# Turning stream chunks with two VectorE operations and four transfers, and combining a down pair's shared products at its end

## Chip, cores, metric

The kernel runs on one core of a Trainium2 chip. The metric is the device time of one execution in microseconds; the profile is one execution taken by the hardware profiler, and its span is the core's time from the first to the last instruction.

## What is computed

A two-layer decoder trunk on 256 tokens of width 2048, all in float32. Layer 0 is differential attention, layer 1 attention over a shared latent; each is followed by an MLP. Cut to what matters here:

```python
x = x + diff_attention(rms_norm(x, a_norm_g[0]), ...) # ends in "o @ w_o"
x = x + sq_relu_mlp(rms_norm(x, mlp_norm_g[0]), w_up[0], w_down[0])
k_nope, k_rope, v = shared_latent_kv(x, kv_in_norm_g, w_dkv, kv_norm_g, w_ukv, cos_b, sin_b)
x = x + mla_attention(rms_norm(x, b_norm_g[0]), ...) # ends in "o @ w_o"
x = x + sq_relu_mlp(rms_norm(x, mlp_norm_g[1]), w_up[1], w_down[1])
return rms_norm(x, final_norm_g)

def sq_relu_mlp(h, w_up, w_down):
    return jnp.square(jax.nn.relu(h @ w_up)) @ w_down
```

## The kernel before

**Products.** Every float32 factor is split in two parts of fewer bits, high and low, and a product is three matmuls: high by high, high by low, low by high (`half_tok`, lines 582 to 584; in `seven`, lines 815 to 817). ScalarE writes the high parts of the weights (`whi`, line 1067), VectorE the low ones (`wlo`, line 1669) from what SyncE's queue loads into the four slots of `raw`. A *block* is 2048 rows by 512 columns of weights; it is cut into eight *halves* of 256 rows, each 12 matmuls of 512 columns (two chunks, two token tiles, three products). `whi` and `wlo` form a ring of four halves. ScalarE may split half hf once TensorE has done half hf - 4, VectorE follows ScalarE, TensorE waits for VectorE (`lo_ready`), and a slot of `raw` is loaded again once VectorE has split it. `body(b, asides)` is the loop that both engines run over the splits: half 3 of block b to half 2 of the next, numbered 3 to 10; `asides` says after which of them other work stands.

**The MLP.** Its 8192 hidden columns are done in four quarters of four up blocks and four down blocks. The sums go to the PSUM tiles `acc`; the squares of the result are turned to become the next operand (`opB`). In all quarters but the edges, blocks 2 and 3 of a down projection (`pair`) and pairs of up blocks (`up_pair`) form part of the result with seven products instead of eight (`seven`, names `B22`, `T1`, `B21`, `B11`, `T2`, `T3`, `T4` in this order, 6 matmuls each). These need sums of weights, which VectorE forms (lines 2197, 2200, 2207, 2213), and their high and low parts (`extra_hi`, `extra_lo`, lines 1389, 1393, 2180, 2186). Four products are shared between results and go to the `side` banks; ScalarE copies them out (lines 1414 for a down pair, 1440 for an up pair), and VectorE combines them with four operations (`combine`, line 2103). For a down pair the result is then scaled and added to the stream `xs` (`down_add`, line 2251, two operations of 1024 columns). The order in one quarter is: down blocks 0 and 1, `pair`, first `up_pair`, second `up_pair`. In the second one, VectorE has the squares of the first to sum and turn (lines 2109, 2117, 2085) and their low parts to write (`hid_low`, line 2093) between the seven products' parts; ScalarE squares (lines 1352, 1360, 1347), moves the turned quadrants with four transfers (`move_quads`, line 1333) and writes high parts (line 1323).

**Stream chunks.** The stream `xs` has tokens on the partitions; the next projection needs it with features there. After a block of an output projection or of the last down projection has been added to `xs` (line 2060, or 2134), its 512 columns (a *chunk*) are turned. VectorE's `transpose` turns squares of 32 by 32, so `turn` (line 1690) issues one operation for each pair of 32-partition groups, 16 a chunk; `x_turn` does them in three parts of 4, 8 and 4, the first behind the addition, the others behind the splits of halves 3 and 4 of the next block (`x_turned_over`). Then, behind half 6, ScalarE writes the chunk's high part to `opA` (`x_hi`, lines 1098 and 1101) and VectorE the low part (`x_lo`, lines 1709 and 1714). There are twelve chunks: four for each output projection and four for layer 0's last down projection. The last chunk of each four is wanted by TensorE at half 6 of the block that follows (`opA_ready`): the first up block of either layer, and the latent projection `B_DKV`.

```python
for a in tokens:
    for c in range(4):
        rows, cols = (slice(32 * k, 32 * k + 32) for k in (a, c))
        done = nc.vector.transpose(
            dest[cols].rearrange("p f (t n) -> p f t n", t=TT)[:, :, :, rows],
            src[rows].rearrange("p t (f n) -> p f t n", f=4)[:, :, :, cols])
```

Of the kernel before, what the change touches and what calls it, by code (L numbers as in the profile page):

```python
# [159 lines left out]
def trunk(nc, x, positions, a_w_qkv, a_lambda, a_w_o, w_dkv, w_ukv, b_w_dq, b_w_uq, b_w_o, w_up, w_down,  # L160
# [11 lines left out]
    with ExitStack() as ctx:  # L172
# [81 lines left out]
        x_turned = o_sb[:].rearrange("p a t n -> p (a t) n")  # L254
        squares = junk[:].rearrange("p a n -> p (a n)").rearrange("p (q c r) -> p q c r", c=4, r=32)
        sq_quads = o_sb[:].rearrange("p a t n -> p (a t n)")
        sq_moved = prob[:].rearrange("p m k -> p (m k)")[:, 0:4 * SEQ].rearrange("p (t a x) -> p t a x", t=TT, a=4)
        sqT = sq_moved.rearrange("p t a (f n) -> p f (t a) n", f=4)
# [55 lines left out]
        x_turns = sem("x_turns")  # L314
        xT_hi = sem("xT_hi")
# [723 lines left out]
        def _(act):  # L1039
# [267 lines left out]
            def out_proj(b0, uses, v0, gain):  # L1307

                x_squares(v0, 1, uses[1] + 1)
                for j in range(1, JB):  # L1310
                    s = (j + 1) % 2
                    body(b0 + j, {6: lambda: x_hi(v0 + j - 1, gain)})
# [4 lines left out]
            def mlp(l, v_in, v_out, nxt, squares_from):  # L1317
# [8 lines left out]
                def move_quads(q, j):  # L1326
# [5 lines left out]
                    for a in range(4):  # L1332
                        act.dma_start(sq_moved[:, :, a, :], sq_quads[32 * a:32 * a + 32, :]).then_inc(sq_moves, 16)  # L1333
# [63 lines left out]
                def pair(q):  # L1397
# [9 lines left out]
                    for hf in range(3):  # L1407
                        split(b + 2, hf)

                def up_pair(q, i, after):  # L1410

                    b = B_MLP[l] + 2 * JB * q + 2 * i
                    def down_copy(k):
                        fn(down_shared[k], side[k], ACT.Copy).then_inc(shared_copied, 1)

# [3 lines left out]
                    elif after == "down":  # L1419
                        down_copy(0)  # L1420
# [3 lines left out]
                    elif after == "down":  # L1424
                        down_copy(1)
# [33 lines left out]
                body(B_MLP[l], {6: lambda: x_hi(v_in + JB - 1, G_MLP[l]), 9: lambda: form_high(x_forms[0], FORM_SETS * l)})  # L1459
# [1093 lines left out]
```

## Time and profile before

| | |
|---|---|
| median of 3 runs (lowest to highest) | 1999.61 us (1997.5 to 1999.82) |
| the profiled execution | 1997.04 us, span 1995.2 us |
| TensorE matmul / weight load busy | 99% / 83% |
| VectorE / ScalarE busy | 82% / 58% |
| DMA | 398.91 MB, mean 200 GB/s |
| granted TensorE clock | 0.999 |

Busy time of a matmul overlaps the next one's, and its end is modelled: a 512-column matmul is shown with 0.39 us while the next starts 0.23 us after it. Idle time is therefore read from the starts.

### The profile page before, as it was taken

To read this page: it belongs to the slowest core of one execution; us is meant where nothing else is said; L and a number is where in the kernel's file an instruction comes from. 1 tells how busy PE (TensorE), PEld (TensorE's weight loads), DVE (VectorE), ACT (ScalarE), POOL (GpSimd) and SP (SyncE) were. 2 spreads that over 40 slices of the span, in tenths; PEclk is the share of its full clock that TensorE was granted. 3 is DMA by queue.
4 is the path that set the end of the run, shared out by engine and by line. 5 is a ranking of instruction groups with operands and counts; after the bars stand their busy time and mean duration, and the time that the engine had idled before them with its cause. 6 is when DMAs were issued, how large, how long until landed. Compare 5 with 4: busy or idle time off the path is not lost.

```text
span 1995.2 us, 26053 instructions
## 1 busy us (share of the span) xinstructions
PE 1981.0 (99%) x9128; PEld 1649.4 (83%) x9128; DVE 1636.8 (82%) x2099; ACT 1155.7 (58%) x1481; POOL 13.2 (1%) x21
## 2 busy tenths in 40 slices
PE   9999999999999999999999999999999999999998
PEld 7888888888888888888878998888887888888887
DVE  7789998977887898788788787977798788789865
ACT  6555555556566556556646665556456556655653
POOL 0000000000000000000000000000000000000000
PEclk9999999999999999999999999999999999999999
DMA  8655545566666566656655554576556656655673
GB/s 309 208 171 188 187 157 181 201 205 227 210 204 214 195 205 225 220 203 196 231 190 173 142 151 148 184 232 216 182 196 227 228 203 207 219 193 200 220 238 108
DMA packets 252861, 398.91 MB, mean 200 GB/s; under 512 B 17648, under 2 KB 75376, under 8 KB 252784
## 3 DMA queue, kind: packets, MB, share of 16 engines
q1 hardware_dynamic: 217104, 379.03, 56.8%
q10 hardware_dynamic: 35680, 18.88, 3.5%
q8 instruction: 44, 0.72, 0.1%
q14 instruction: 33, 0.27, 0.0%
HBM read 379.00 MB, written 2.10 MB: 191 GB/s over the span
## 4 chain that ended last, share of the span: by engine, by line
PE 80%; DVE 8%; issue 5%; ACT 3%; ACTq 2%; DMA 1%; SPq 0%; DVEq 0%; POOLq 0%; POOL 0%
PE acc L582 20%; PE acc L584 20%; PE acc L583 20%; PE acc L602 2%; PE acc L604 2%; PE acc L603 2%; DVE wlo L1669 2%; PE side L815 2%; PE side L817 2%; PE side L816 2%; ACTq L1333 2%; DVE wlo L2186 1%; PE acc L815 1%; PE acc L817 1%; PE acc L816 1%
## 5 line engine op out<-in xcount | busy, mean ns | idle before, releaser
L1669 DVE TENSOR_TENSOR wlo<-raw,whi 128x1024 fp32r<-128x1024 f32 (+1 forms) x596 | 708.1, 1206 | 158.8 <-ACT whi L1067 156.7
L1067 ACT ACTIVATE whi<-raw 128x1024 fp32r<-128x1024 f32 (+1 forms) x596 | 608.3, 1044 | 392.0 <-PE acc L584 267.4
L582 PE MATMUL acc<-whi,opB 128*128 128x512 f32 x1104 | 431.1, 390 | 1.3 <-DVE wlo L1669 1.2
L584 PE MATMUL acc<-whi,opB 128*128 128x512 f32 x1104 | 429.8, 389 | 0.0
L583 PE MATMUL acc<-wlo,opB 128*128 128x512 f32 x1104 | 429.5, 389 | 0.0
L582 PE MATMUL acc<-whi,opA 128*128 128x512 f32 (+2 forms) x1072 | 414.7, 387 | 0.0
L584 PE MATMUL acc<-whi,opA 128*128 128x512 f32 (+2 forms) x1072 | 414.0, 386 | 0.0
L583 PE MATMUL acc<-wlo,opA 128*128 128x512 f32 (+2 forms) x1072 | 413.8, 386 | 0.0
L582 PEld LDWEIGHTS acc<-whi,opB 128*128 128x128 f32 x1104 | 207.3, 188 | 44.8 <-DVE wlo L1669 2.4
L584 PEld LDWEIGHTS acc<-whi,opB 128*128 128x128 f32 x1104 | 207.2, 188 | 43.3
L583 PEld LDWEIGHTS acc<-wlo,opB 128*128 128x128 f32 x1104 | 207.3, 188 | 42.7
L584 PEld LDWEIGHTS acc<-whi,opA 128*128 128x128 f32 x1072 | 201.3, 188 | 40.3
L582 PEld LDWEIGHTS acc<-whi,opA 128*128 128x128 f32 x1072 | 201.3, 188 | 40.1 <-issue 0.4
L583 PEld LDWEIGHTS acc<-wlo,opA 128*128 128x128 f32 x1072 | 201.4, 188 | 39.8
L1393 ACT ACTIVATE whi<-raw 128x1024 fp32r<-128x1024 f32 x78 | 82.6, 1059 | 79.5 <-issue 28.7
L2186 DVE TENSOR_TENSOR wlo<-raw,whi 128x1024 fp32r<-128x1024 f32 x78 | 95.1, 1220 | 16.6 <-ACT whi L1393 16.6
L1389 ACT ACTIVATE extra_hi<-raw 128x1024 fp32r<-128x1024 f32 x52 | 54.7, 1051 | 74.1 <-PE side L817 74.1
L1690 DVE STREAM_TRANSPOSE o_sb<-xs 32x256 f32<-32x256 f32 x192 | 83.8, 436 | 3.3
L2085 DVE STREAM_TRANSPOSE o_sb<-junk 128x1024 f32<-128x1024 f32 x32 | 39.8, 1245 | 44.1 <-ACT junk L1347 43.8
L2180 DVE TENSOR_TENSOR extra_lo<-raw,extra_hi 128x1024 fp32r<-128x1024 f32 x52 | 63.5, 1221 | 13.8 <-ACT extra_hi L1389 13.6
L602 PE MATMUL acc<-whi,opA 128*128 128x512 f32 x184 | 71.8, 390 | 0.2 <-DVE wlo L1669 0.2
L603 PE MATMUL acc<-wlo,opA 128*128 128x512 f32 x184 | 71.7, 389 | 0.0
(379 smaller groups left out, 2431.1 us busy)
## 6 DMA issues: line engine op xcount, KB each, us to landing
raw<-in_w_up SPq DMA_DIRECT2D x128, 1024.0 KB, 5.4
raw<-in_w_down SPq DMA_DIRECT2D x128, 1024.0 KB, 5.0
raw<-in_a_w_qkv SPq DMA_DIRECT2D x44, 1024.0 KB, 5.1
raw<-in_a_w_o SPq DMA_DIRECT2D x16, 1024.0 KB, 5.0
prob<-o_sb ACTq DMA_DIRECT2D x128, 128.0 KB, 2.9
raw<-in_b_w_o SPq DMA_DIRECT2D x16, 1024.0 KB, 5.0
raw<-in_w_ukv SPq DMA_DIRECT2D x32, 256.0 KB, 4.1
raw<-in_w_dkv SPq DMA_DIRECT2D x4, 1024.0 KB, 5.0
```

What stands on the lines that cost most here:

```text
L582: mm(o, a_hi, w_hi, start=start, stop=False)
L583: mm(o, a_hi, w_lo, start=False, stop=False)
L584: done = mm(o, a_lo, w_hi, start=False, stop=last and c == chunks - 1)
L602: mm(o, a_hi, whi[:, place, :], start=start, stop=False)
L603: mm(o, a_hi, wlo[:, place, :], start=False, stop=False)
L815: mm(o, a_hi, hi[:, place + c, :], start=first and c == 0, stop=False)
L1067: done = fn(whi[:, place:place + ch, 0:n], raw[:, r, c0:c0 + ch, 0:n], ACT.Copy)
L1393: fn(whi[:, 2 * (hf % 4):2 * (hf % 4) + 2, :], source[f], ACT.Copy).then_inc(hi_ready, 1)
L1669: done = tt_(wlo[:, place:place + ch, 0:n], raw[:, r, c0:c0 + ch, 0:n], whi[:, place:place + ch, 0:n].bitcast(F32), ALU.subtract)
L1690: done = nc.vector.transpose(dest[cols].rearrange("p f (t n) -> p f t n", t=TT)[:, :, :, rows], src[rows].rearrange("p t (f n) -> p f t n" ...
L2180: tt_(extra_lo[:, places, :], src, extra_hi[:, places, :].bitcast(F32), ALU.subtract).then_inc(extra_lo_ready, 1)
L2186: tt_(wlo[:, places, :], src, whi[:, places, :].bitcast(F32), ALU.subtract).then_inc(lo_ready, 1)
```

## The change

A chunk is now turned by two VectorE operations over all 128 partitions, one for each token tile. They turn every 32 by 32 square in its place of four partition groups and read `xs` with a step of four columns, so that each group of 32 partitions ends up with whole quadrants (`quads`, in `o_sb`). Four transfers issued by ScalarE (`x_move`) bring the groups to their columns in `prob` (`quads_moved`, read as `sqT`), the same way and through the same two buffers as the hidden squares are moved. High and low parts read from there. All of the turning stands behind the addition; `x_move` stands behind half 4 and the high and low parts behind half 7 (in block 1 of the last down projection behind 7 and 10). In the first up block the high and low parts of the forms of `x` go to the block after.

The four copies of a down pair's shared products are issued behind the second of the three splits that end `pair`, no longer between the splits of the next up pair. VectorE's `combine` stands at the end of `pair`, ahead of the last addition, and `down_add` behind the first sum of the next up pair, ahead of the split of half 4.

```diff
+            def x_move(v):
+
+                act.wait_ge(x_turns, v - JB + 1)
+                act.wait_ge(xT_lo, 4 * v)
+                for a in range(4):
+                    act.dma_start(quads_moved[:, :, a, :], quads[32 * a:32 * a + 32, :]).then_inc(x_moves, 16)
+
             def x_hi(v, gain):
 
-                act.wait_ge(x_turns, v - JB + 1)
+                act.wait_ge(x_moves, 64 * (v - JB) + 64)
                 c = JB * (v % JB)
+                high = opA[:, c:c + 4, 0, :].rearrange("p f (a n) -> p f a n", n=32)
                 if gain is None:
-                    fn(opA[:, c:c + 4, 0, :], x_turned, ACT.Copy).then_inc(xT_hi, 4)
+                    fn(high, sqT, ACT.Copy).then_inc(xT_hi, 4)
                     return
                 for k in range(4):
-                    fn(opA[:, c + k, 0, :], x_turned[:, k, :], ACT.Copy,
+                    fn(high[:, k], sqT[:, k], ACT.Copy,
                        scale=gains[:, gain + c + k:gain + c + k + 1]).then_inc(xT_hi, 1)
...
                     seven(down_groups(l, q, 1), 2, b + 1, 2, (1, b + 1), (2, b + 1), {})
                     split(b + 1, 6)
                     split(b + 1, 7)
-                    for hf in range(3):
-                        split(b + 2, hf)
+                    split(b + 2, 0)
+                    split(b + 2, 1)
+                    for k in range(4):
+                        fn(down_shared[k], side[k], ACT.Copy).then_inc(shared_copied, 1)
+                    split(b + 2, 2)
...
                     split(b, 5)
-                    if after == "down":
-                        down_copy(2)
-                    else:
+                    if after != "down":
                         move_quads(q, 2 * i - 1)
-                    between = {"B22": lambda: down_copy(3)} if after == "down" else {
-                        "B21": lambda: hid_high(q, 2 * i - 1)}
+                    between = {} if after == "down" else {"B21": lambda: hid_high(q, 2 * i - 1)}
...
-            def x_turn(v, tokens, s, added):
+            def x_turn(v, s, added):
 
                 dve.wait_ge(drained[s], added)
+                if not (isinstance(v, int) and v == JB):
+                    dve.wait_ge(x_moves, 64 * (v - JB))
                 j = v % JB
-                done = turn(x_turned, xs[:, :, NB * j:NB * j + NB], tokens)
-                if 3 in tokens:
-                    done.then_inc(x_turns, 1)
+                for t in range(TT):
+                    done = nc.vector.transpose(
+                        quads.rearrange("p (c t f n) -> p t f c n", c=4, t=TT, n=32)[:, t],
+                        xs[:, t, NB * j:NB * j + NB].rearrange("p (f r c) -> p f c r", f=4, c=4))
+                done.then_inc(x_turns, 1)
...
+                    combine(down_shares(l, q), down_shared)
                     add_scaled(b + 1, 0, 2 * uses[0], slice(3 * NB, 4 * NB))
...
                 def down_add(q):
 
                     dve.wait_ge(shared_sums, 4 * down_shares(l, q) + 4)
+                    for side_bank in range(2):
+                        dve.wait_ge(drained[side_bank], 2 * (u[side_bank] + U_QUARTER * q + U_UP + 2))
...
-                        if follows != "down":
+                        if follows == "down":
+                            down_add(q - 1)
+                        else:
                             up_turn(q, 2 * i - 1)
...
-                    split(b + 1, 2)
-                    if follows == "down":
-                        down_add(q - 1)
-                    for hf in range(3, 6):
+                    for hf in range(2, 6):
                         split(b + 1, hf)
                     combine(up_shares(l, q, i), up_shared)
...
-                body(B_MLP[l], {**x_turned_over(v_in + JB - 1, G_MLP[l], 0, 2 * u[0]),
-                                7: lambda: stream_stats(2 * l + 1, True), 8: x_form_sums,
-                                10: lambda: form_low(x_forms, FORM_SETS * l)})
-                body(B_MLP[l] + 1, {3: lambda: up_turn(0, 0), 6: lambda: hid_low(0, 0)})
+                body(B_MLP[l], {7: lambda: x_lo(v_in + JB - 1, G_MLP[l]), 8: lambda: stream_stats(2 * l + 1, True),
+                                9: x_form_sums})
+                body(B_MLP[l] + 1, {3: lambda: up_turn(0, 0), 4: lambda: form_low(x_forms, FORM_SETS * l), 6: lambda: hid_low(0, 0)})
```

TensorE's instructions and their order are the same in both kernels. On VectorE, around the addition of block 1 of layer 0's last down projection (`xs<-acc`), before:

```order
L2134 SCALAR_TENSOR_TENSOR xs<-acc,rs,xs 128x512 x2
L1690 STREAM_TRANSPOSE o_sb<-xs 32x8x32 x4
L1669 TENSOR_TENSOR wlo<-raw,whi 128x1024
L1690 STREAM_TRANSPOSE o_sb<-xs 32x8x32 x8
L1669 TENSOR_TENSOR wlo<-raw,whi 128x1024
L1690 STREAM_TRANSPOSE o_sb<-xs 32x8x32 x4
L1669 TENSOR_TENSOR wlo<-raw,whi 128x1024 x2
L1709 TENSOR_TENSOR opA<-o_sb,opA 128x4x256
L1669 TENSOR_TENSOR wlo<-raw,whi 128x1024 x4
```

and now:

```order
L2135 SCALAR_TENSOR_TENSOR xs<-acc,rs,xs 128x512 x2
L1704 STREAM_TRANSPOSE o_sb<-xs 128x4x4x32 x2
L1671 TENSOR_TENSOR wlo<-raw,whi 128x1024 x5
L1715 TENSOR_TENSOR opA<-prob,opA 128x4x256
L1671 TENSOR_TENSOR wlo<-raw,whi 128x1024 x3
```

The 16 transposes between splits have become two behind the addition, and the low part of the chunk (`opA`) stands one split later. On VectorE at the end of a down pair and in the up pair behind it (`o_sb<-o_sb,junk` is the first of the four combining operations, `xs<-junk` and `xs<-o_sb` are the two additions of the combined products, `attn_both<-raw` is the first sum), before:

```order
L1669 TENSOR_TENSOR wlo<-raw,whi 128x1024
L2131 ISA
L2134 SCALAR_TENSOR_TENSOR xs<-acc,rs,xs 128x512 x2
L1657 ISA
L1669 TENSOR_TENSOR wlo<-raw,whi 128x1024
...
L2197 TENSOR_TENSOR attn_both<-raw 128x1024
...
L2097 ISA
L2103 TENSOR_TENSOR o_sb<-o_sb,junk 128x512
...
L1669 TENSOR_TENSOR wlo<-raw,whi 128x1024
L2251 SCALAR_TENSOR_TENSOR xs<-junk,rs,xs 128x1024
L2251 SCALAR_TENSOR_TENSOR xs<-o_sb,rs,xs 128x1024
```

and now:

```order
L1671 TENSOR_TENSOR wlo<-raw,whi 128x1024
L2098 ISA
L2104 TENSOR_TENSOR o_sb<-o_sb,junk 128x512
...
L2132 ISA
L2135 SCALAR_TENSOR_TENSOR xs<-acc,rs,xs 128x512 x2
L1659 ISA
L1671 TENSOR_TENSOR wlo<-raw,whi 128x1024
...
L2198 TENSOR_TENSOR attn_both<-raw 128x1024
L2247 ISA x2
L2250 SCALAR_TENSOR_TENSOR xs<-junk,rs,xs 128x1024
L2250 SCALAR_TENSOR_TENSOR xs<-o_sb,rs,xs 128x1024
```

The combining has moved ahead of the last addition from `acc`, and the two additions from behind the seven products' parts to behind the first sum. On ScalarE at the same place (`junk<-side` and `o_sb<-side` are the copies), before:

```order
L1067 ACTIVATE whi<-raw 128x1024
L1414 ACTIVATE junk<-side 128x512
L1056 REGISTER_ALU
L1067 ACTIVATE whi<-raw 128x1024
L1414 ACTIVATE junk<-side 128x512
L1056 REGISTER_ALU
L1067 ACTIVATE whi<-raw 128x1024
L1414 ACTIVATE o_sb<-side 128x512
```

and now:

```order
L1067 ACTIVATE whi<-raw 128x1024
L1056 REGISTER_ALU
L1067 ACTIVATE whi<-raw 128x1024
L1418 ACTIVATE junk<-side 128x512 x2
L1418 ACTIVATE o_sb<-side 128x512 x2
L1056 REGISTER_ALU
L1067 ACTIVATE whi<-raw 128x1024
```

The four copies now stand together ahead of one split.

## Rows read from the trace of the kernel before

**Rows 1.** The page, busy time by engine; then the waits of TensorE (total, times, longest).

```profile
PE 1981.0 (99%) x9128; PEld 1649.4 (83%) x9128; DVE 1636.8 (82%) x2099; ACT 1155.7 (58%) x1481; POOL 13.2 (1%) x21
...
PE side L815 <- DVE wlo L2186: 3.7, 6, 0.6
PE acc L582 <- DVE wlo L1669: 1.2, 1, 1.2
```

**Rows 2.** Timeline, TensorE, last down projection of layer 0 (start, duration, operation).

```profile
1031.29 0.39 PE L583 MATMUL acc<-wlo,opB 128*128 128x512 f32 x1
1031.52 0.39 PE L584 MATMUL acc<-whi,opB 128*128 128x512 f32 x1
1033.09 0.50 PE L582 MATMUL acc<-whi,opB 128*128 128x512 f32 x1 [1.18 <-DVE wlo L1669]
...
1035.71 0.39 PE L584 MATMUL acc<-whi,opB 128*128 128x512 f32 x1
1036.17 0.50 PE L582 MATMUL acc<-whi,opB 128*128 128x512 f32 x1
```

**Rows 3.** Timeline, VectorE, the same stretch.

```profile
1028.21 3.58 DVE L1690 STREAM_TRANSPOSE o_sb<-xs 32x256 f32<-32x256 f32 x8
1031.80 1.23 DVE L1669 TENSOR_TENSOR wlo<-raw,whi 128x1024 fp32r<-128x1024 f32 x1
...
1034.89 2.36 DVE L1669 TENSOR_TENSOR wlo<-raw,whi 128x1024 fp32r<-128x1024 f32 x2
```

**Rows 4.** Timeline, TensorE, second up pair of quarter 1, layer 0.

```profile
612.81 0.40 PE L817 MATMUL acc<-whi,opA 128*128 128x512 f32 x1
613.16 0.50 PE L815 MATMUL side<-extra_hi,opA 128*128 128x512 f32 x1
...
614.45 0.39 PE L817 MATMUL side<-extra_hi,opA 128*128 128x512 f32 x1
615.43 0.50 PE L815 MATMUL side<-whi,q_parts 128*128 128x512 f32 x1 [0.60 <-DVE wlo L2186]
615.77 0.39 PE L816 MATMUL side<-wlo,q_parts 128*128 128x512 f32 x1
```

**Rows 5.** Timeline, VectorE, both up pairs of that quarter.

```profile
575.23 1.28 DVE L2251 SCALAR_TENSOR_TENSOR xs<-o_sb,rs,xs 128x1024 f32<-128x1024 f32 x1
...
579.84 0.69 DVE L2103 TENSOR_TENSOR junk<-junk 128x512 f32<-128x512 f32 x1
...
622.95 0.69 DVE L2103 TENSOR_TENSOR junk<-junk 128x512 f32<-128x512 f32 x1 [0.72 <-ACT prob L1440]
```

**Rows 6.** Timeline, ScalarE, last copy of shared products in either up pair.

```profile
578.80 0.61 ACT L1440 ACTIVATE prob<-side 128x512 f32<-128x512 f32 x1
...
622.31 0.61 ACT L1440 ACTIVATE prob<-side 128x512 f32<-128x512 f32 x1
```

**Rows 7.** Groups of instructions (line, shapes, busy us and mean ns, idle before).

```profile
L1690 DVE STREAM_TRANSPOSE o_sb<-xs 32x256 f32<-32x256 f32 x192 | 83.8, 436 | 3.3
L2085 DVE STREAM_TRANSPOSE o_sb<-junk 128x1024 f32<-128x1024 f32 x32 | 39.8, 1245 | 44.1 <-ACT junk L1347 43.8
...
L1352 ACT ACTIVATE junk<-o_sb 128x1024 f32<-128x1024 f32 x14 | 28.8, 2054 | 27.0 <-DVE o_sb L2109 27.0
```

**Rows 8.** Timeline, TensorE, first matmul of the first up pair.

```profile
550.14 0.39 PE L582 MATMUL acc<-whi,opA 128*128 128x512 f32 x1
```

**Rows 9.** Timeline, VectorE, start of the first up pair.

```profile
550.51 1.41 DVE L2134 SCALAR_TENSOR_TENSOR xs<-acc,rs,xs 128x512 f32<-128x512 f32 x2 [0.56 <-PE acc L584]
...
554.38 1.23 DVE L2197 TENSOR_TENSOR attn_both<-raw 128x1024 f32<-128x1024 f32 x1 [1.33 <-DMA raw<-in_w_up]
```

**Rows 10.** Instructions on tile prob: the transfers, durations min/median/max.

```profile
L1333 ACTq DMA_DIRECT2D prob<-o_sb x128: 617/642/1553, 407.6 to 1911.8; - x128
...
DMA to landing us min/median/max: 2.6/2.9/6.0
```

**Rows 11.** The page, costliest groups: ScalarE's high parts.

```profile
L1067 ACT ACTIVATE whi<-raw 128x1024 fp32r<-128x1024 f32 (+1 forms) x596 | 608.3, 1044 | 392.0 <-PE acc L584 267.4
```

More of the change, by code:

```diff
@@ L314, in trunk @@
         x_turns = sem("x_turns")
+        x_moves = sem("x_moves")
         xT_hi = sem("xT_hi")
@@ L1311, in out_proj @@
                     s = (j + 1) % 2
-                    body(b0 + j, {6: lambda: x_hi(v0 + j - 1, gain)})
+                    body(b0 + j, {4: lambda: x_move(v0 + j - 1), 7: lambda: x_hi(v0 + j - 1, gain)})
                     x_squares(v0 + j, s, uses[s] + j // 2 + 1)
@@ L1418, in up_pair @@
                         square_second(q, i - 1)
-                    elif after == "down":
-                        down_copy(0)
                     split(b, 4)
@@ L1526, in latent_hi @@
                        scale=gains[:, gain + c:gain + c + 1]).then_inc(latT_hi, 1)
-            body(B_DKV, {6: lambda: x_hi(V_MLP0 + JB - 1, None)}, kind="dkv", nxt="rq")
+            body(B_DKV, {4: lambda: x_move(V_MLP0 + JB - 1), 7: lambda: x_hi(V_MLP0 + JB - 1, None)}, kind="dkv", nxt="rq")
             latent(0, B_DKV, 1, stage, KV_LORA, 0)
@@ L1693, in turn @@
                 return done
-            def x_turn(v, tokens, s, added):
+            def x_turn(v, s, added):
                 dve.wait_ge(drained[s], added)
+                if not (isinstance(v, int) and v == JB):
+                    dve.wait_ge(x_moves, 64 * (v - JB))
                 j = v % JB
-                done = turn(x_turned, xs[:, :, NB * j:NB * j + NB], tokens)
-                if 3 in tokens:
-                    done.then_inc(x_turns, 1)
+                for t in range(TT):
[3 more added lines that the diff above has]
+                done.then_inc(x_turns, 1)
             def x_lo(v, gain):
-                dve.wait_ge(x_turns, v - JB + 1)
                 c = JB * (v % JB)
+                high, low = (opA[:, c:c + 4, i, :].rearrange("p f (a n) -> p f a n", n=32) for i in range(2))
                 if gain is None:
                     dve.wait_ge(xT_hi, 4 * v + 4)
-                    tt_(opA[:, c:c + 4, 1, :], x_turned, opA[:, c:c + 4, 0, :].bitcast(F32),
-                        ALU.subtract).then_inc(xT_lo, 4)
+                    tt_(low, sqT, high.bitcast(F32), ALU.subtract).then_inc(xT_lo, 4)
                     return
@@ L1713, in x_lo @@
                     dve.wait_ge(xT_hi, 4 * v + k + 1)
-                    stt(out=opA[:, c + k, 1, :], in0=x_turned[:, k, :], scalar=gains[:, gain + c + k:gain + c + k + 1],
-                        in1=opA[:, c + k, 0, :].bitcast(F32), op0=ALU.mult, op1=ALU.subtract).then_inc(xT_lo, 1)
-            def x_turned_over(v, gain, s, added):
-                return {3: lambda: x_turn(v, (1, 2), s, added), 4: lambda: x_turn(v, (3,), s, added),
-                        6: lambda: x_lo(v, gain)}
+                    stt(out=low[:, k], in0=sqT[:, k], scalar=gains[:, gain + c + k:gain + c + k + 1],
+                        in1=high[:, k].bitcast(F32), op0=ALU.mult, op1=ALU.subtract).then_inc(xT_lo, 1)
             def stream_stats(t, squared):
@@ L2207, in seven @@
                     tt_(b22, w_sum, b22, ALU.add).then_inc(w_summed, 1)
-                    if "third sum" in after:
-                        after["third sum"]()
                     low("B21", group, at, b, hf0, b21)
@@ L2268, in up_pair @@
                     after = {"first sum": after_first, "second sum": lambda: split(b, 5)}
-                    if follows == "down":
-                        after["third sum"] = lambda: down_combine(q - 1)
-                    else:
+                    if follows != "down":
                         after["B11"] = lambda: hid_low(q, 2 * i - 1)
                     seven(up_groups(l, q, i), i - 1, b, 6, (3, b), (0, b + 1), 8 * b + 3, after)
-                    split(b + 1, 2)
-                    if follows == "down":
-                        down_add(q - 1)
-                    for hf in range(3, 6):
+                    for hf in range(2, 6):
                         split(b + 1, hf)
```

43 lines of the change are left out of this document (18 added, 25 removed).

## Prediction

> **What bounds the kernel now.** I read the page first and then every wait of TensorE, because an engine that is busy 99% of the span leaves others almost nothing to give [rows 1]. TensorE's waits in total come to under 7 us in 1995.2: six of 0.6 us on VectorE's line 2186 and one of 1.2 us on line 1669 carry nearly all of it [rows 1]. So the question is not how much work the change takes off VectorE, but what it does to these seven places and whether it makes a new one.
>
> Busy time hides short holes, so I took the starts of the matmuls in TensorE's timeline. A 512-column matmul starts 0.23 us after the one before. I list every step longer than 0.30 us; beyond the regular 0.23 they add up to 11.1 us, in two kinds of place that the change touches, with 8.3 us, and in the start and the attention stages, which it leaves alone.
>
> The first kind is one place, in the third column block of layer 0's last down projection. The matmul after 1031.52 starts 1.57 us later, so 1.34 are lost; a half further on 0.46 lie between two starts, so 0.23 [rows 2]. After such a hole the next step is also 0.33 to 0.34 long instead of 0.23, as [rows 4] show. Together 1.34 + 0.23 + 2 x 0.1 = 1.8 us. The cause is in VectorE's timeline: eight transposes of 32 partitions run from 1028.21, and the low parts (line 1669) that TensorE wants start only at 1031.80; the next pair of them stands behind four more transposes, at 1034.89 [rows 3].
>
> The second kind occurs six times, once for each quarter but the last in each layer, in the second up pair. There TensorE loses 0.12 us at the product B11 (612.81 to 613.16), 0.75 us at T2 (614.45 to 615.43), and 0.11 us in the step behind each (615.43 to 615.77) [rows 4]: 1.1 us each time, 6.5 in all.
>
> I followed the chain of waits back from this hole: VectorE's own operations, ScalarE behind four transfer issues, the sums and squares of the pair before, and so on to line 2103 at 579.84 [rows 5], where VectorE puts together the shared products of the first up pair. That operation is the anchor. ScalarE's last copy of those products ends at 578.80 + 0.61 = 579.41 [rows 6], but VectorE starts only at 579.84, since its three splits are behind the two additions of line 2251, the second of which starts at 575.23 [rows 5]. In the second up pair, where no such additions stand ahead, the same operation starts at 622.95, 0.03 after its last copy's end at 622.31 + 0.61 = 622.92, and the row says that it waited for this copy [rows 5, 6].
>
> **The change, part by part.** *Turning a stream chunk.* Twelve chunks are turned. Before, each took 16 transposes of 436 ns: 192 of them, 83.8 us [rows 7]. Now each takes two of 128 x 512. The trace has none; the nearest is line 2085, 128 x 1024 in 1245 ns [rows 7], half of which is 0.62. The new ones read their source with a step of four elements. Line 1352 reads so on ScalarE and takes 2054 ns for 1024 columns [rows 7], where two copies of 512 take 0.61 each [rows 6], so the upper bound is twice, 1.25. I take 0.62, because the nearest row is the same operation: 24 x 0.62 = 15 us (30 at the upper bound), 69 us less on VectorE. Of this only the hole of 1.8 us is on the path. The low parts at 1031.80 have no transposes ahead of them any more except two right behind the additions, so both that hole and the one behind it go: **minus 1.8 us**.
>
> *The four transfers.* Each chunk adds four issues on ScalarE, 0.64 us each, and they land 2.9 us after the issue (median; 6.0 at most) [rows 10]. The 48 issues hold ScalarE 31 us in all. They lie behind the split of half 4, and each block gives ScalarE 8 halves x 12 matmuls x 0.227 = 21.8 us for 8 splits of 1.04 [rows 11], squares and one high part, so 2.6 us more are covered. The Trainium skill, DMA: Bandwidth & Descriptors, Issuing engines are not separate DMA queues, has the issuing time as usually small relative to the DMA itself; the trace does not agree here, 2.6 us of issues against a landing of 2.9, and by that rule the risk that the issues hold the splits up would be none. What could be late is the high part, moved from half 6 to 7, and the low part behind it. TensorE needs the last chunk at half 6 of the following block, 16.3 us after the block's start, in three places only (the first up block of both layers and the latent projection). Split 7 can start when four halves are done, at 10.9; the split ends at 12.0, the high parts at 13.7 and the low parts at about 15.2 (my estimate: one operation of 1024 columns takes 1.04 and 1.23 us [rows 3, 11], and cut in four some 1.7). The transfers are issued by 7.2 and landed by 10, with the slowest landing by 12.6. So about 1 us is left: **0**. If the slowest landing fell there, it would cost half a us at one place.
>
> *The shared products of the down pair.* ScalarE's four copies, VectorE's four combining operations (4 x 0.69 = 2.8 us) and two additions (1.28 each) leave the middle of the first up pair. The combining goes ahead of the pair's last addition, the two additions behind the first sum. The total work stays, so the gain is one of order. From the anchor on nothing is ahead of line 2103 but ScalarE's copies, so it starts at 579.44 and the chain behind it is 0.40 earlier. Each link further down is an operation that waits for the one before (VectorE, ScalarE, issues), none for TensorE. The weights that the next first sum wants are fetched when a split of the same chain frees their slot, so they come earlier too. T2's hole shrinks by what the chain gains; TensorE arrives 0.23 earlier as B11's hole goes. Hence 1.1 becomes 0.7, and 6 x 0.40 = **minus 2.4 us**. Bounds: 0, if another releaser ends the chain's waits at the same time as now, and 6.5, if all of the holes go.
>
> *What stands in the way at the pair's start.* VectorE is free at 549.95 (it idles 0.56 before 550.51) [rows 9], and the copies delay its third split by about 0.15. Then come combining 2.8, an addition 1.33, a split 1.14: it reaches the first sum at 555.4, after the weights for which it waited until 554.38 [rows 9]. So the idle time of 1.33 there is the cover. With the sum (1.14), the two additions (2.4) and a split of 1.22 the low parts of half 4 are ready at 560.1. TensorE starts the block at 550.14 [rows 8] and comes to half 4 after 4 x 12 x 0.23 = 11.0 us, at 561.2. The margin is 1.1 us; every later half has more. **0**.
>
> *Moved in the first up block.* The forms' high and low parts (1.05 and 1.2 us) go one block later, where drain and first move have slack: 0.
>
> **Sum.** 1.8 + 2.4 = 4.2 us off the profiled execution, 1997.04, gives 1992.8. The median of the three runs shown is 1999.61, 2.6 above that execution; against it the forecast is 1995.4. A measurement of this kernel tells about 0.2% (4.0 us) from no change, so the forecast lies right at this edge.
>
> **Rivals.**
> *Only the chunk's hole goes (1997.8).* For: two transfers' landings and a weight fetch lie in the chain beside the operations, and if either does not come 0.40 earlier, nothing is gained. Against: the DMA issues follow the chain's own operations. 13%.
> *All holes go (1991.3).* 8.3 us, if the chain comes earlier by over 1 us, as it would where ScalarE, without copies between its splits, runs ahead more than I see. Against: the anchor waits for TensorE's seven products and cannot be earlier than 579.4. 12%.
> *A new wait at the pair's start (2003.8, slower).* The place is half 4 of the first up pair. The price is 6 times what VectorE is late beyond 1.1 us; 0.7 us too late eats the gain (6 x 0.7 = 4.2), and from there the kernel is slower. If the first sum's weights land at 557.8 instead of 554.4 [rows 9], half 4 is ready at 562.6, 1.4 too late: 6 x 1.4 = 8.4, less 4.2. For: the cover at this place, 1.33 us of idle time, is used up. Against: the split that frees the weights' slot stands ahead of the combining, so nothing postpones their fetch. 7%.
> *The change doesn't do what it says (1999.6).* ScalarE is held in `x_move` by the issues and by waiting for the transposes, and splits fall behind by as much as VectorE got ahead. For: four issues of 0.64 stand in a queue that splits share. Against: ScalarE sits idle for 267 us of the span in front of its splits, waiting for TensorE to free their places [rows 11]. 6%.
> *VectorE was the bound (1931).* TensorE's weight loads are busy 83% and VectorE 82% [rows 1]; were the matmuls stretched by waiting inside their busy time, the 69 us would come off in full. Against: the starts are 0.23 apart with holes of 11.1 us in all. 2%. The Trainium skill, Perfetto Trace Analysis, Identifying the Most-Contended Engine, has matmul busy time as a bad measure and weight-load busy share as the good one for the room left; by that rule TensorE has room and the time would be nearer to 1931, and here the starts of the matmuls decide against it.
>
> **From cases to numbers.** The forecast gets 60%. It lies at the edge and three runs scatter by 2.3 us, so I split it 35 to 25 over faster and same. Faster: 35 + 12 + 2 = 49%. Same: 25 + 13 + 6 = 44%. Slower: 7%. The range reaches from the case in which all holes go, 1991.3, to just above the case in which only the chunk's hole goes, 1999.0; outside are the slower case, the one without effect, VectorE's and some scatter, 2 in 10.
>
> **What would show it.** Right: no step over 0.30 us near 1031; 24 transposes of 128 x 512 at 0.62 to 1.25; the combining of the first up pair starts 0.03 after the fourth copy; T2's wait is about 0.45 instead of 0.60 by the profile, and B11's step is back at 0.23. Wrong: a wait of TensorE on line 1671 at half 4 of the first up pair or at half 6 of a block that takes a chunk; T2's hole unchanged or gone.

## The result and the profile after

The changed kernel takes 2003.6 us (median of 8 runs, 2002.84 to 2005.96) against 1999.11 for the kernel before (8 runs, 1997.5 to 1999.82) on the same chip. The ratio is 1.0024, 95% interval 1.0014 to 1.0033. It is slower by 4.5 us, where 1995.4 was forecast. The profiled execution took 2005.96 us, its span is 2004.2.

The page's lines on the span, on busy time and on queue q14 (packets, MB, share of 16 engines), kernel after:

```profile
span 2004.2 us, 25960 instructions
...
PE 1985.4 (99%) x9128; PEld 1653.1 (82%) x9128; DVE 1578.2 (79%) x1931; ACT 1156.6 (58%) x1481; POOL 13.2 (1%) x21
...
q14 instruction: 42, 0.34, 0.0%
```

VectorE lost 168 instructions, as planned, and 58.6 us of work, where the prediction had 69 [rows 1]. The time rose. TensorE's waits say where, kernel after:

```profile
PE acc L582 <- DVE opB L2094: 4.4, 2, 2.2
PE side L815 <- DVE wlo L2187: 3.7, 6, 0.6
...
PE side L815 <- DVE extra_lo L2181: 0.8, 1, 0.8
PE acc L582 <- DVE wlo L1671: 0.7, 2, 0.4
```

The 1.2 us on the chunk's low parts [rows 1] is gone. The six waits at T2 are all there and as long as before, which the prediction had named as a sign of being wrong. New are two waits of 2.2 us for `opB` (line 2094, `hid_low`). They stand in layer 0, at the start of the second and the third pass of the loop over the quarters. TensorE's timeline at the first of them, kernel after:

```profile
647.76 0.39 PE L584 MATMUL acc<-whi,opB 128*128 128x512 f32 x1
650.38 0.49 PE L582 MATMUL acc<-whi,opB 128*128 128x512 f32 x1 [2.23 <-DVE opB L2094]
...
651.63 0.62 PE L584 MATMUL acc<-whi,opB 128*128 128x512 f32 x1
652.05 0.63 PE L582 MATMUL acc<-whi,opB 128*128 128x512 f32 x1
...
654.61 0.60 PE L582 MATMUL acc<-whi,opB 128*128 128x512 f32 x1
655.04 0.40 PE L583 MATMUL acc<-wlo,opB 128*128 128x512 f32 x1
```

The step is 2.62 instead of 0.23. From 651.63 to 655.04 eight steps are 0.43 long instead of 0.23: behind the idle time TensorE ran for 3.4 us at the lower of its two levels, 1.2 GHz. That costs another 8 x 0.2 = 1.6. The windows view (span, then busy time of the engines; the seventh figure is the granted clock, then DMA share and GB/s) shows it too:

```profile
640.00:660.00 20.00, 17.46 (x69) 13.66 (x68) 10.22 (x10) 10.03 (x11) 0.00 (x0) 0.91 0.56 174
```

All steps over 0.30 us ("long steps" from here on), beyond 0.23 each and without those of the first 20 us, add up to 19.4 us after and 11.1 before. The two places hold 4.6 + 4.6 = 9.2 of it. Of the rest, 1.8 us went near 1031 and 0.9 came in the second up pairs. These 8.3 us account for the two profiled executions, which lie 8.9 apart (1997.04 and 2005.96); the medians lie only 4.5 apart, because the one profiled execution is 2.1 below its median and the other 2.4 above. What differs between an execution and its median, no trace shows.

**Why VectorE is late there.** Its timeline, kernel after:

```profile
637.07 1.23 DVE L1671 TENSOR_TENSOR wlo<-raw,whi 128x1024 fp32r<-128x1024 f32 x1 [1.76 <-ACT whi L1067]
642.66 0.69 DVE L2118 TENSOR_TENSOR attn_both<-acc,attn_both 128x512 f32<-128x512 f32 x1 [4.36 <-PE acc L584]
```

The same two instructions in the kernel before:

```profile
636.61 1.23 DVE L1669 TENSOR_TENSOR wlo<-raw,whi 128x1024 fp32r<-128x1024 f32 x1 [1.75 <-ACT whi L1067]
637.75 0.68 DVE L2117 TENSOR_TENSOR attn_both<-acc,attn_both 128x512 f32<-128x512 f32 x1
```

The low part is the last operation of a pass, the sum (line 2118) the first of the next: between them VectorE jumps back (line 2291). Before, the jump cost nothing (1.14 from start to start, as between any two such operations). Now VectorE does nothing from 638.3 to 642.66. The row puts this on TensorE's `acc`. The chain that ended last tells it otherwise (start, length, what; `DVEq` is VectorE's own handling of register and branch instructions), kernel after:

```profile
635.98 1.07 ACT whi L1067
...
637.16 0.07 DVEq L2291
637.23 5.18 issue
642.41 0.09 DVEq L2291
...
642.66 0.70 DVE attn_both L2118
```

"issue" is time in which the engine waited for nothing that the profile shows. The branch of the jump runs at 637.16, and the next instruction, a register operation that needs nothing of TensorE, only at 642.41. The DMA view of 636 to 652 us has one queue more than that of the kernel before:

```profile
q14 instruction: 3, 0.02, 0.5%
```

In this window the kernel before has no such packet. Queue q14 brings instructions, 8 KB in a packet (0.34 MB in 42 of them; before 33). The three lie at 640.6, 643.0 and 645.5 us, about 2.5 us apart. The work after the jump is a chain of sum, squares, turning, transfers, high and low part, and everything in it is late by the pause. At 812.5 us it happens again; in layer 1, whose loop has the same body, it doesn't (1568.61 to 1569.75).

### The profile page after: what moved, and what is told of

Same layout as the page of the kernel before. It is cut to its first block, busy times and chain, and to the rows that moved or that the text cites. A ratio compares the mean times of both kernels' runs of the same rounds, so it can differ in the third digit from the quotient of the medians.

```text
span 2004.2 us, 25960 instructions
## 1 busy us (share of the span) xinstructions
PE 1985.4 (99%) x9128; PEld 1653.1 (82%) x9128; DVE 1578.2 (79%) x1931; ACT 1156.6 (58%) x1481; POOL 13.2 (1%) x21
## 4 chain that ended last, share of the span: by engine, by line
PE 83%; ACT 4%; issue 4%; DVE 4%; DMA 2%; ACTq 2%; SPq 0%; DVEq 0%; POOLq 0%; POOL 0%
PE acc L582 20%; PE acc L584 20%; PE acc L583 20%; PE side L815 2%; PE side L816 2%; PE side L817 2%; PE acc L602 2%; PE acc L603 2%; PE acc L604 2%; DMA prob<-o_sb 2%; ACTq L1341 2%; PE acc L815 2%; PE acc L817 2%; PE acc L816 1%; ACT whi L1067 1%
## 5 line engine op out<-in xcount | busy, mean ns | idle before, releaser
L602 PE MATMUL acc<-whi,opA 128*128 128x512 f32 x184 | 71.8, 390 | 0.2 <-DVE wlo L1671 0.2
L604 PE MATMUL acc<-whi,opA 128*128 128x512 f32 x184 | 71.7, 390 | 0.0
```

The lines of the kernel that those rows point to most:

```text
L602: mm(o, a_hi, whi[:, place, :], start=start, stop=False)
L604: done = mm(o, a_lo, whi[:, place, :], start=False, stop=end)
```

## The experiments

**Theory 1**: at the jump back part of VectorE's loop is no longer in its instruction store (the place from which the engine reads its program) and is fetched again. The change put the loop elsewhere, because 16 transposes a chunk became 2 and all instructions behind them moved up. **Theory 2**: the change's own work (four copies, combining, transfers at other places) makes VectorE late. In each experiment both kernels ran on one chip; "before" is its median there. Line numbers of the variants are shifted by a few.

| kernel | us (runs) | before, us (runs) | ratio, 95% interval |
|---|---|---|---|
| changed + 24 memsets | 1994.69 (11) | 1998.76 (26) | 0.998, 0.9971 to 0.9989 |
| before + 72 memsets | 2014.93 (5) | 1998.76 (26) | 1.0077, 1.0063 to 1.0091 |
| down pair's part only | 1997.27 (11) | 1998.76 (26) | 0.9991, 0.9982 to 1.0 |
| chunks' part only | 2004.25 (10) | 1998.76 (26) | 1.0025, 1.0015 to 1.0034 |
| chunks' part + 24 memsets | 1997.02 (11) | 1999.1 (16) | 0.9989, 0.998 to 0.9998 |
| before + 36 memsets | 2008.19 (5) | 1999.45 (13) | 1.0046, 1.0032 to 1.0059 |
| changed, loop written out | 1994.46 (9) | 1999.45 (13) | 0.9977, 0.9967 to 0.9987 |
| changed + 24, low part later | 1991.14 (5) | 1999.45 (13) | 0.9961, 0.9947 to 0.9974 |
| changed + 24, both later | 1989.9 (5) | 1999.45 (13) | 0.9951, 0.9938 to 0.9965 |
| before, both later | 1993.26 (6) | 1999.1 (16) | 0.997, 0.9958 to 0.9982 |
| changed, loop written out, both later | 1989.96 (5) | 1999.1 (16) | 0.9952, 0.9938 to 0.9966 |

### The changed kernel, moved by 24 places

```diff
             nc.vector.memset(junk[:, 0, 0:P], 0.0).then_inc(zeros_ready, 1)
+            for k in range(24):
+                nc.vector.memset(junk[:, 1, k:k + 1], 0.0)
             for c in range(FIRST):
```

> The changed kernel with 24 one-column memsets at the start of VectorE's program, so that every later instruction of VectorE stands 24 places further on. Theory 1 (code fetch): VectorE's loop over the quarters has about 277 instructions, and where it stands decides how much of it has to be fetched again at the jump back; TensorE waits 2.2 us for VectorE there, twice, and runs at the lower clock behind it, about 9 us together. 24 places further on the two waits are gone: 2003.6 - 9 = 1994.6 us, no packets of the instruction queue between 600 and 840 us. Theory 2 (the work): the waits come from what the change does in the second up pair (four copies, combining, transfers at other places); 24 memsets alter none of it: 2003.6.

Measured: 1994.69 us, 8.9 less than the changed kernel. The two were not measured side by side; each against the kernel before on its own chip, one is 4.5 above and the other 4.1 below, 8.6 apart. Its two longest waits of TensorE in the waits view, and the page's line on its instruction queue:

```profile
PE side L815 <- DVE wlo L2189: 3.6, 6, 0.6
PE side L635 <- DVE junk L1826: 1.1, 1, 1.1
```

```profile
q14 instruction: 32, 0.26, 0.0%
```

The two waits of 2.2 are gone, and no instruction packet lies between 602 and 843 us. Added instructions that do nothing useful made the kernel faster by 9 us. Theory 2 cannot say why.

### The kernel before, moved by 72 places

The same edit with 72 memsets in the kernel before.

> The kernel before, its work as it was, with 72 memsets at the start of VectorE's program, so that layer 0's loop over the quarters begins at place 660 where it began at 588 (in the changed kernel at 532; 660 is 532 + 128). Theory 1 (code fetch, in blocks of 128 instructions): the kernel before gets the two waits at the jump back too: 1999.1 + 9 = 2008, with packets of the instruction queue at 640 to 650 us and at 815 to 825. Theory 2 (the work): no part of the change is in it, so 1999.1 and at most 1 more for the memsets.

Measured: 2014.93 us, 16.2 more. The waits of TensorE:

```profile
PE acc L582 <- DVE opB L2095: 8.9, 4, 2.2
PE side L815 <- DVE wlo L2188: 3.7, 6, 0.6
PE acc L582 <- DVE wlo L1669: 2.2, 4, 1.2
```

Theory 1 holds: the old work, at another place, gets the same wait. The forecast of 2008 missed, since there are four waits and not two: layer 1's loop has them as well. My places were the cause of the miss. They were taken from the program's listing, in which a loop has 276 instructions and begins at 532 or 588. The trace's own records of VectorE, register and semaphore instructions included, have 299 from one jump back to the next, 301 with the change. Beginnings of the loops worked out from these records replace the others from here on.

### The two parts of the change, each alone

`down_only` has the diff's changes in `pair`, `up_pair` and `down_add`, and the old turning of chunks; `chunks_only` is the rest of the diff: `x_turn`, `x_move`, `x_hi`, `x_lo` and their places.

> Only the down pair's part of the change: the four copies at the pair's end, the combining ahead of the last addition, the two additions behind the first sum. Layer 0's loop begins where it began before (place 588). Theory 1 (code fetch): no wait at the jump back; T2's hole stays as it is since the transfers of the chain land no earlier: 1998.5 to 1999.5. Rival, forecast as the new wait at the pair's start: if this part is what costs, 2003 to 2005 here. My term of minus 2.4 would give 1996.7.

> Only the stream chunks' part of the change (two transposes and four transfers a chunk, forms one block later); the shared products as before. Layer 0's loop begins at place 532 as in the changed kernel. Theory 1 (code fetch): the two waits at the jump back come with this part, and the hole near 1031 goes: 1999.1 + 9 - 1.8 = 2006.3, or with the changed kernel's 2003.6 if the down pair's part gives anything. If the down pair's part were the cause instead: 1997.3.

Measured: 1997.27 and 2004.25 us. TensorE's longest waits, of `down_only` and then of `chunks_only`:

```profile
PE side L815 <- DVE wlo L2179: 3.5, 6, 0.6
PE acc L582 <- DVE wlo L1662: 1.2, 1, 1.2
```

```profile
PE acc L582 <- DVE opB L2101: 4.5, 2, 2.3
PE side L815 <- DVE wlo L2194: 3.6, 6, 0.6
PE side L815 <- DVE extra_lo L2188: 1.9, 4, 0.7
```

The down pair's part costs nothing. It gives 1.5 us, between the 2.4 of my term and the 0.3 and less of theory 1's expectation, and the interval holds both. The two waits come with the chunks' part, which changes no instruction of the second up pair.

### The chunks' part, moved by 24 places

> Only the stream chunks' part of the change, with the 24 memsets, so that no loop begins where four blocks are needed (592 and 1368 of VectorE's stream, 80 and 88 modulo 128). My term for this part, the hole near 1031: 1.8 us off, so 1999.0 - 1.8 = 1997.2, and no wait at the jump back. If the four transfers or the later high and low parts cost something of their own, it is over 1999.

Measured: 1997.02 against 1999.1, so 2.1 less; no wait for `opB` is left. The interval reaches from 0.4 to 4.0 us, and it holds the term of 1.8. The trace shows the hole near 1031 gone, but not that it is the whole effect: the profiled execution took 1997.53, against 1997.04 before, and the long steps of the six second up pairs are 8.7 us, against 7.0 before. In these pairs B11's step is 0.56 to 0.83 long, where it was 0.34 to 0.37 in five of six before; why, no run shows.

With the down pair's 1.5 the medians make 3.6, where the changed kernel with 24 memsets has 4.1 less than before. So the medians add up within what can be measured. The long steps in the second up pairs do not: 7.0 before, 6.8 with the down pair's part, 8.7 with the chunks' part and 24 memsets, 6.2 with both parts and 24 memsets, each by one profile.

### Where a loop may begin

> The kernel before with 36 memsets. By the records of the traces layer 0's loop over the quarters takes 299 instructions, layer 1's as many, and they begin at 625 and 1510 of VectorE's stream (in the changed kernel 568 and 1347). If instructions are fetched in blocks of 128 of which three stay, a loop of 299 needs four blocks for 43 of 128 beginnings. Beginnings modulo 128 so far: 46, 56, 57 with waits at the jump back; 65, 67, 80, 91, 102, 104, 113 without. Here they are 21 (layer 0) and 10 (layer 1). By this model layer 0 gets two waits and layer 1 none: 1998.8 + 8 = 2007. If it is the sheer number of added instructions: four waits, 2013. If it is the alignment that the changed kernel happens to share with the 72 memsets alone: 1998.8.

Measured: 2008.19, 8.7 more. VectorE at the first jump back of layer 0, then of layer 1:

```profile
637.17 1.23 DVE L1669 TENSOR_TENSOR wlo<-raw,whi 128x1024 fp32r<-128x1024 f32 x1 [1.75 <-ACT whi L1067]
643.90 0.69 DVE L2119 TENSOR_TENSOR attn_both<-acc,attn_both 128x512 f32<-128x512 f32 x1 [5.50 <-issue]
...
1570.62 1.23 DVE L1669 TENSOR_TENSOR wlo<-raw,whi 128x1024 fp32r<-128x1024 f32 x1 [1.75 <-ACT whi L1067]
1571.77 0.68 DVE L2119 TENSOR_TENSOR attn_both<-acc,attn_both 128x512 f32<-128x512 f32 x1
```

Layer 0 has the pause and layer 1 has none, as the model of blocks says. Here the profile itself names "issue" in place of TensorE. All beginnings together:

| kernel | layer 0: begins, mod 128, waits | layer 1: begins, mod 128, waits |
|---|---|---|
| before | 625, 113, 0 | 1510, 102, 0 |
| changed | 568, 56, 2 | 1347, 67, 0 |
| changed + 24 | 592, 80, 0 | 1371, 91, 0 |
| before + 72 | 697, 57, 2 | 1582, 46, 2 |
| before + 36 | 661, 21, 2 | 1546, 10, 0 |
| down pair only | 625, 113, 0 | 1512, 104, 0 |
| chunks only | 568, 56, 2 | 1345, 65, 0 |
| chunks + 24 | 592, 80, 0 | 1369, 89, 0 |

Waits come at 21, 46, 56 and 57 and at none of 10 and 65 to 113. A loop of 299 to 301 needs four blocks of 128 instructions for 42 to 44 of 128 beginnings and three for the others (the forecast above says 43). One stretch of that width, which begins between 14 and 21, fits all sixteen. That a packet of 8 KB holds 128 instructions is inferred too: the kernel with the loop written out (below) has 404 instructions more in VectorE's program than the changed kernel with 24 memsets, and three packets more, 35 against 32, so about 135 each. The model rests on its fit and on the one forecast above, not on a view of the store.

The Trainium skill, Advanced Engine Details and Errata, ISA Cache, has the instruction cache as 32 KB in two lines of 256 instructions each. By it a loop of 299 to 301 would need a third line for 42 to 44 of 256 beginnings. The trace does not agree. Modulo 256 the beginnings with waits are 56, 185, 46 and 149, and no stretch of 44 holds them. The packets carry 8 KB, not 16. The total of 32 KB would fit four blocks of 8 KB, if three stay while a fourth is being fetched; no run shows how many the store holds.

### The loop written out

```diff
-                with dve.Fori(0, QUARTERS - 1) as q:
+                for q in range(QUARTERS - 1):
```

> The changed kernel, no memsets, with VectorE's loop over the quarters written out three times for each layer, so that its stream has no jump back there (the other engines keep theirs). Theory 1 (code fetch at the jump back): a stream that only runs forward is fetched ahead in time; no waits at 640 and 815 us: 1994.7. Theory 2 (the work): 2003.6. If fetching itself is too slow even forward, more and scattered waits: over 2003.6.

Measured: 1994.46. The place of the former jump back, VectorE's timeline:

```profile
637.31 1.23 DVE L1671 TENSOR_TENSOR wlo<-raw,whi 128x1024 fp32r<-128x1024 f32 x1 [1.76 <-ACT whi L1067]
638.45 0.68 DVE L2118 TENSOR_TENSOR attn_both<-acc,attn_both 128x512 f32<-128x512 f32 x1
```

1.14 again, and no pause of this kind is left. The forward stream was fetched in time: its 35 instruction packets, against the changed kernel's 42, cost TensorE nothing. So here the fetch costs only where it begins after the jump. Writing the loop out also takes register instructions away (VectorE's records fall from 3103 to 2327), so this run alone would not tell these from the jump; the runs with memsets do, since they keep all of them.

### The hole at T2

The other miss is T2's hole, which did not shrink. VectorE and TensorE in the changed kernel with 24 memsets (`extra_lo` is B11's low part, `opB` is `hid_low`, `wlo` T2's low part; line 815 opens B11 and then T2):

```profile
611.98 1.23 DVE L2183 TENSOR_TENSOR extra_lo<-raw,extra_hi 128x1024 fp32r<-128x1024 f32 x1 [0.23 <-ACT extra_hi L1397]
...
613.12 1.22 DVE L2096 TENSOR_TENSOR opB<-prob,opB 128x1024 fp32r<-128x1024 f32 x1
...
613.25 0.50 PE L815 MATMUL side<-extra_hi,opA 128*128 128x512 f32 x1
...
614.25 1.22 DVE L2189 TENSOR_TENSOR wlo<-raw,whi 128x1024 fp32r<-128x1024 f32 x1
...
615.53 0.51 PE L815 MATMUL side<-whi,q_parts 128*128 128x512 f32 x1 [0.62 <-DVE wlo L2189]
```

TensorE starts B11 when its low part ends. T2's low part ends two operations later, 2 x 1.14 = 2.3 us. TensorE has six matmuls in between, the first with the long step: 1.5. The difference, 0.8, is the hole, whatever the chain in front does, as long as B11's low part comes no earlier than TensorE.

> The changed kernel with the 24 memsets, and in each second up pair VectorE's low part of the moved quadrants (hid_low) stands behind the low part of T4, no longer between those of B11 and T2. Theory A: T2's hole of 0.6 is the time of this operation, since VectorE has three operations from B11's low part to T2's (3 x 1.14 us from start to end of the third) against TensorE's six matmuls, whenever the first of them comes late; so the six holes at T2 go: 1994.7 - 6 x 0.7 = 1990.5, with B11's step as it is. Theory B (the chain as I forecast it: T2 waits for whatever the whole chain releases last, here the transfers' landing): a hole of the same size stays at T2 or moves to T3 or T4: 1994.7.

```diff
                    low("B11", group, at, b, hf0, b11)
-                    if "B11" in after:
-                        after["B11"]()
                    low("T2", group, at, b, hf0, b22)
...
                    low("T4", group, at, b, hf0, w_sum)
+                    if "T4" in after:
+                        after["T4"]()
...
-                        after["B11"] = lambda: hid_low(q, 2 * i - 1)
+                        after["T4"] = lambda: hid_low(q, 2 * i - 1)
```

Measured: 1991.14, which is 3.6 below the same kernel without this edit on another chip, and 4.2 if each is taken against the kernel before on its own chip. The same stretch now:

```profile
611.85 1.23 DVE L2183 TENSOR_TENSOR extra_lo<-raw,extra_hi 128x1024 fp32r<-128x1024 f32 x1 [0.34 <-ACT extra_hi L1397]
612.99 1.22 DVE L2189 TENSOR_TENSOR wlo<-raw,whi 128x1024 fp32r<-128x1024 f32 x1
...
613.13 0.50 PE L815 MATMUL side<-extra_hi,opA 128*128 128x512 f32 x1
...
614.39 0.40 PE L817 MATMUL side<-extra_hi,opA 128*128 128x512 f32 x1
614.62 0.40 PE L815 MATMUL side<-whi,q_parts 128*128 128x512 f32 x1
```

From 614.39 to 614.62 it is 0.23: the hole is gone. The long steps of the seven products in the six second up pairs fall from 6.2 us to 2.1. Theory A holds: no step at T2 is long any more, and what is left stands mostly at B11 and the product before it in layer 1's first pass.

> As low_later, and ScalarE's high part of the moved quadrants (hid_high) stands behind the high part of T2, no longer behind that of B21, so that ScalarE doesn't wait for the landing of the transfers ahead of B11. Theory A: B11's step of 0.31 to 0.54 and the one behind it go too: 1990.5 - 6 x 0.3 = 1988.7. If the landing had nothing to do with B11's late parts: as low_later.

```diff
-                    between = {} if after == "down" else {"B21": lambda: hid_high(q, 2 * i - 1)}
+                    between = {} if after == "down" else {"T2": lambda: hid_high(q, 2 * i - 1)}
```

Measured: 1989.9, 1.2 over what was expected. The six pairs' long steps are 1.4 us, nearly all in layer 1's first. Against the run without this edit that is 1.2 less with overlapping intervals, so what the edit adds isn't settled.

### The same idea without the change, and a version without places

> The kernel before, without any part of the change, with hid_high behind T2's high part on ScalarE and hid_low behind T4's low part on VectorE in each second up pair. If T2's holes come from this order alone and not from what the change moves, they go here as well: 6.9 us of long steps in the six pairs fall to about 1.4, 1999.0 - 5.5 = 1993.5. If the earlier combining of the change is needed for that: 1997 or more.

Measured: 1993.26. What the two moved operations give (5.8 us) doesn't need the change. The six pairs' long steps are 1.9 us, where 1.4 was expected, and no wait at T2 is left. All long steps together fall from 11.1 to 6.2, so they account for 4.9 of the 5.8.

> The changed kernel with VectorE's loop over the quarters written out (no memsets) and both parts of the quadrants later. Nothing depends on where the loop begins, and the holes at T2 are gone: 1994.5 - 4.8 = 1989.7. Below both kernels, by 14 us and 9 us.

Measured: 1989.96 us (1989.5 to 1990.39), 9.1 below the kernel before and 13.6 below the changed one (measured on another occasion). Its waits of TensorE, all of them:

```profile
PE side L635 <- DVE junk L1826: 1.1, 1, 1.1
PE side L815 <- DVE extra_lo L2181: 0.6, 1, 0.6
PE acc L602 <- DVE wlo L1671: 0.3, 1, 0.3
```

## Why the prediction was wrong, step by step

Two steps failed. The sum had no term for the place of the code behind the removed instructions, which cost 8.9 us and made the kernel slower instead of faster. And T2's hole did not shrink as the chain came earlier: its six waits stayed at 0.6 each, where the term took 0.40 off each of six holes. Step by step:

**What bounds the kernel** held: TensorE's few waits, not VectorE's busy share, set the time. 58.6 us less work on VectorE gave no more than the holes. But six waits on line 2186 and one on line 1669 do not carry "nearly all" of the waits: they are 3.7 + 1.2 = 4.9 of 6.7 us, and one of 1.1 on line 1825 stands beside them.

**Turning a chunk, minus 1.8** held as far as it can be told: the hole is gone from the trace, and 2.1 was measured alone (0.4 to 4.0). The transposes were mis-sized:

```profile
L1704 DVE STREAM_TRANSPOSE o_sb<-xs x24: 1049/1092/1120, 316.4 to 1312.8; 128x512 f32<-128x512 f32 x24
```

1.09 us each where I took 0.62; the bound of 1.25 held. Whether the step of four or a fixed part in each operation makes the difference wasn't tried. It opened no hole near 1031, where the whole effect was expected.

**The four transfers, 0** held as far as TensorE's waits tell: none names `opA` in the changed kernel. The prediction's 2.6 us of issues against a landing of 2.9 set four issues beside one landing. One against one it is 0.64 to 2.9 [rows 10], so this row is not at odds with the page that the prediction cites there.

**The down pair, minus 2.4**: the size can't be told from what was measured (1.5, interval 0 to 3.6), but the place was wrong. What was foreseen at the anchor came: the combining started 0.04 after the fourth copy's end (579.40 + 0.61 = 580.01), row of the kernel after:

```profile
580.05 0.69 DVE L2104 TENSOR_TENSOR junk<-junk 128x512 f32<-128x512 f32 x1 [0.72 <-ACT prob L1441]
```

From that copy's start the transfers were issued 602.47 - 579.40 = 23.07 us later, against 602.25 - 578.80 = 23.45 before: 0.38 earlier, as forecast. But the high part that waits for their landing started 610.34 - 579.40 = 30.94 later, against 609.73 - 578.80 = 30.93 [rows 6]. ScalarE's row, before and then after:

```profile
609.73 1.06 ACT L1323 ACTIVATE opB<-prob 128x1024 fp32r<-128x1024 f32 x1 [1.66 <-DMA prob<-o_sb]
```

```profile
610.34 1.06 ACT L1331 ACTIVATE opB<-prob 128x1024 fp32r<-128x1024 f32 x1 [2.02 <-DMA prob<-o_sb]
```

So in this pair the chain's gain was lost in the transfers' landing, the lower bound that I had written down and given 13% as a rival. The slowest of the four transfers landed 5.8 us after its issue, against 5.5 before, with a median of 2.7 in both; what holds it back wasn't tried. The step that failed is "T2's hole shrinks by what the chain gains". Even where the chain came earlier, the gain went to B11's steps, and T2's wait stayed at 0.6, because `hid_low` stands between the two low parts. The rows of all three operations were there, and I did not compare VectorE's distance with TensorE's. The long steps of the six pairs are 7.0 us before, 6.8 with this part alone and 6.2 in the changed kernel with 24 memsets: 0.2 and 0.8 less, where 2.4 was forecast.

**The pair's start, 0** held. VectorE reached half 4 at 559.51 and its low part ended at 560.73, where I had 560.1; TensorE doesn't wait there, and the first sum's weights were there when VectorE came.

**What was missing** is the 9 us. I gave 7% to a slower case of 2003.8, and the time came out at 2003.6, by coincidence: its mechanism, a wait at half 4 of the first up pair, did not occur. No term of the sum asked what the removed instructions do to the place of those behind them. The change takes some 160 instructions out of VectorE's stream, 57 of them ahead of layer 0's loop, whose beginning moves from 625 to 568. The page of the kernel before showed that instructions are fetched by DMA in the run (33 packets on q14), so the question could have been asked. Without this effect the median is 4.1 less with 24 memsets (1994.69, forecast 1995.4), close to the sum of 4.2. That is luck in part. The interval reaches from 2.2 to 5.8, and the traces account for only 2.2: the profiled execution with 24 memsets took 1994.91 against 1997.04, and its long steps add up to 8.9 us against 11.1. Of that 1.8 is the chunk's hole and 0.8 lies in the second up pairs, not 2.4; some 0.4 elsewhere goes the other way. With the effect it is 8.9 more: 2003.6.

## What to carry to other kernels

When an edit changes how many instructions stand ahead of a long loop of an engine, look at the first operation after the jump back before blaming the work: a pause of several us with "issue" in the chain and packets on the instruction queue point to a fetch. It can be tested with a few idle instructions ahead of the loop, and avoided by writing the loop out. When two engines work through the same list, compare for each pair of neighbours how long either takes; an operation of something else in between makes a hole of fixed size as long as the first of the pair comes late; moving that operation removes it.

## What the runs showed of the hardware

A loop of about 300 instructions on VectorE repeats free of cost or with 4.2 to 5.5 us of pause at each jump back, by its place alone: 9 us for two pauses, 16 for four. In the changed kernel the 8 KB packets of such a fetch came about 2.5 us apart (640.6, 643.0, 645.5). There the row's releaser (TensorE's `acc`) was wrong, and only the chain showed "issue". A wait of 2.2 us on TensorE cost up to 1.6 more at the lower clock, for the 3.4 us behind it.
